# Splitting weights fewer tiles ahead in the mixers of a three-layer transformer on one core, with two gate steps a beat later and a shorter pooling matmul

## The reference

```python
for l in range(2):
    x = x + 0.5 * swiglu(rms_norm(x, ffn1_norm), ffn1_w_gate_up, ffn1_w_down)   # L0f1, L1f1
    z = rms_norm(x, mix_norm) @ w_in                     # L0, L1: u, q, k, v and two gates
    y_pool = multiscale_pool(u, pool_w, pool_scale)      # means over windows of 2, 4, 8, 16 tokens
    y_attn = attention(rope(rms_norm(q)), rope(rms_norm(k)), v)
    x = x + (gate0 * (y_pool @ w_branch_pool) + gate1 * (y_attn @ w_branch_attn)) @ w_out
    x = x + 0.5 * swiglu(rms_norm(x, ffn2_norm), ffn2_w_gate_up, ffn2_w_down)   # L0f2, L1f2
h = rms_norm(x, norm1_w) @ w_in_2                        # M
hm = mlstm_chunkwise(silu(conv(q, k)), v, i_pre, log_sigmoid(f_pre))   # q, k: Mqk; v: Mmv; mo: Mmo
on = gates * (compressed, selected and window attention)  # compress: 8 tiles Mkw1*, Mvw1*
x = x + (sigmoid(gm) * (hm @ w_up_m) + sigmoid(gn) * (on @ w_up_n)) @ w_out     # Mg, Mbr, Mwo
x = x + (gelu(conv(a)) * v) @ w_down                     # Mf
```

## Time and profile before

| | before |
|---|---|
| median of three runs | 1455.54 us |
| the profiled execution's own time | 1455.04 us |
| its span, first to last instruction | 1453.2 us |
| PE busy | 1441.2 us, 99% |
| DVE busy | 986.5 us, 68% |
| ACT busy | 820.1 us, 56% |
| POOL busy | 144.0 us, 10% |
| granted TensorE clock, mean | 0.999 |

### The profile page before, as it was taken

The page is one execution under the profiler, slowest core; times in us unless marked ns, Lnnn a source line. Parts: engine busy times, 40 slices in busy tenths (PEclk is TensorE's granted clock), DMA queues, the critical chain, the costliest instruction groups (busy, mean ns, idle before and its releaser), DMA issues.

```text
span 1453.2 us, 20919 instructions
## 1 busy us (share of the span) xinstructions
PE 1441.2 (99%) x8064; PEld 1235.0 (85%) x8064; DVE 986.5 (68%) x1604; ACT 820.1 (56%) x1414; POOL 144.0 (10%) x212
## 2 busy tenths in 40 slices
PE   9999999999999999999999999999998999999999
PEld 7888888798888888888887888888887899888887
DVE  6665676766666576666676677666676866778775
ACT  6555556754655555555557646555557665455553
POOL 0100023000000001000050003000049200100000
PEclk9999999999999999999999999999999999999999
DMA  8765555454656647655464456555546343456651
GB/s 330 248 196 195 181 204 181 138 182 169 214 183 193 197 142 234 193 187 191 161 228 159 150 170 216 186 194 186 186 152 249 120 139 132 159 173 220 196 188 51
DMA packets 73683, 267.78 MB, mean 184 GB/s; under 512 B 8176, under 2 KB 8304, under 8 KB 73456
## 3 DMA queue, kind: packets, MB, share of 16 engines
q1 hardware_dynamic: 73296, 265.65, 54.8%
q10 hardware_dynamic: 288, 0.79, 0.1%
HBM read 265.36 MB, written 1.05 MB: 183 GB/s over the span
## 4 chain that ended last, share of the span: by engine, by line
PE 96%; ACT 2%; DVE 1%; DMA 1%; issue 0%; SPq 0%
PE bank L545 29%; PE bank L550 15%; PE bank L498 8%; PE bank L499 8%; PE bank L500 8%; PE bank L559 4%; PE bank L564 4%; PE bank L560 4%; PE bank L528 3%; PE bank L535 3%; PE bank L529 3%; PE bank L518 1%; DMA raw<-w_dram 1%; PE bank L714 1%; PE bank L701 1%; PE bank L690 1%
## 5 line engine op out<-in xcount | busy, mean ns | idle before, releaser
L1558 DVE TENSOR_TENSOR wlo<-raw,whi 128x1024 fp32r<-128x1024 f32 (+1 forms) x481 | 578.5, 1225 | 18.1 <-ACT whi L1029 18.1
L1029 ACT ACTIVATE whi<-raw 128x1024 fp32r<-128x1024 f32 (+1 forms) x481 | 497.8, 1050 | 7.5 <-DMA raw<-w_dram 3.1
L545 PE MATMUL bank<-hx,whi 128*128 128x512 f32 x1856 | 468.7, 393 | 0.0
L545 PEld LDWEIGHTS bank<-hx,whi 128*128 128x128 f32 x1856 | 338.7, 189 | 66.2 <-issue 3.0
L550 PEld LDWEIGHTS bank<-hx,wlo 128*128 128x128 f32 x1856 | 253.3, 191 | 18.2
L550 PE MATMUL bank<-hx,wlo 128*128 128x256 f32 x1856 | 258.9, 283 | 0.0
L498 PE MATMUL bank<-whi,hid 128*128 128x512 f32 x536 | 211.5, 395 | 0.2 <-issue 0.2
L499 PE MATMUL bank<-wlo,hid 128*128 128x512 f32 x536 | 210.1, 392 | 0.0
L500 PE MATMUL bank<-whi,hid 128*128 128x512 f32 x536 | 208.9, 390 | 0.0
L1058 ACT ACTIVATE hid<-prod 128x256 fp32r<-128x256 f32 x126 | 52.7, 418 | 168.9 <-DVE prod L1662 109.0
L500 PEld LDWEIGHTS bank<-whi,hid 128*128 128x128 f32 x536 | 100.8, 188 | 21.8
(11 more groups left out here) (241 smaller groups left out, 1526.8 us busy)
## 6 DMA issues: line engine op xcount, KB each, us to landing
raw<-w_dram SPq DMA_DIRECT2D x486, 512.0 KB, 4.0
gain<-g_dram SPq DMA_DIRECT2D x7, 512.0 KB, 3.8
arena<-c_dram SPq DMA_DIRECT2D x2, 768.0 KB, 6.2
cst<-c_dram SPq DMA_DIRECT2D x1, 1056.0 KB, 6.4
out_dram<-x SPq DMA_DIRECT2D x4, 256.0 KB, 2.0
par<-p_dram SPq DMA_DIRECT2D x1, 867.0 KB, 8.0
raw<-w_dram SPq DMA_DIRECT2D x2, 432.0 KB, 3.6
gain<-g_dram ACTq DMA_DIRECT2D x1, 512.0 KB, 4.7
```

The lines of the kernel that those rows point to most:

```text
L545: e.matmul(b[:, :], hi_of(j)[:, k * P:k * P + P], hx[:, k * 2 * S:k * 2 * S + 2 * S], start=k == 0, stop=False, skip_group_check=True)
L1029: e.activation(hi_of(t), raw_of(t), ACT.Copy).then_inc(sem["w_hi"], 1)
L1558: e.tensor_tensor(lo_of(t), raw_of(t), hi_of(t).bitcast(F32), ALU.subtract).then_inc(sem["w_lo"], 1)
```

## The change

Four things are changed, no others. First, `HI_LEAD` and `LO_LEAD` give the leads tile by tile in the mixers. Second, the forget gates' columns (`gate_cols`) move from beat 29 to beat 30 on PE and DVE, and stand behind the attention of beat 29. Third, the transposes of the compressed attention's weights (`compressed` step 4, PE L913 and ACT L1395) move from beat 43 to 44. Fourth, the first pooling matmul of a group writes 130, 132, 136 or 144 columns in place of 256.

```diff
+MIXED_TILES = [f"Mqk{i}" if kind == "qk" else f"M{'kv'[i // 4]}w1{i % 4}" for kind, i in MIXED]
+HI_LEAD = dict(zip(MIXED_TILES, (3, 6, 6, 4, 3, 2, 1, 1, 3, 2, 2, 2)), Mmv0=2, Mmv2=3)
+LO_LEAD = dict(zip(MIXED_TILES, (3, 5, 5, 4, 3, 2, 1, 0, 1, 2, 1, 1)), Mmv0=1, Mmv2=1)
+for _t in ["Mmv4", "Mmv6"] + [f"Mmo{k}" for k in (0, 2, 4, 6)] + [f"Mg{j}{f}" for f in range(KD) for j in range(2)]:
+    HI_LEAD[_t], LO_LEAD[_t] = 4, 2
+HI_LEAD["Mg17"], LO_LEAD["Mg07"], LO_LEAD["Mg17"] = 5, 3, 4
+for _t in [f"L{l}g{j}{f}" for l in range(2) for f in range(KD) for j in range(2) if f or j]:
+    HI_LEAD[_t], LO_LEAD[_t] = 4, 3
...
-                    e.matmul(b[:, 0:S], us[:, g * P:g * P + P], pm[:, 0:S], start=True, stop=False, skip_group_check=True)
+                    reach = P + 2 ** (g + 1)
+                    e.matmul(b[:, 0:reach], us[:, g * P:g * P + P], pm[:, 0:reach], start=True, stop=False, skip_group_check=True)
...
-                    if beat == 29:
+                    attention(2, beat, 29, js, before)
+                    if beat == 30:
                         gate_cols()
-                    attention(2, beat, 29, js, before)
-                    if beat in (31, 34, 36, 38, 43):
-                        compressed((31, 34, 36, 38, 43).index(beat))
+                    if beat in (31, 34, 36, 38, 44):
+                        compressed((31, 34, 36, 38, 44).index(beat))
...
             def ahead(j):
-                hi_upto(min(j + AHEAD, len(plan) - 1))
+                hi_upto(min(j + HI_LEAD.get(plan[j][0], AHEAD), len(plan) - 1))
...
-                        hi_upto(T[f"Mqk{i}"] + 4)
+                        ahead(T[f"Mqk{i}"])
...
-                lo_upto(min(j + AHEAD - 1, len(plan) - 1))
+                lo_upto(min(j + LO_LEAD.get(plan[j][0], AHEAD - 1), len(plan) - 1))
```

More of the change, by code:

```diff
@@ L1448, in tick @@
                         compressed(3)
-                    if beat == 43:
+                    if beat == 44:
                         compressed(4)
@@ L1501, in mixer2 @@
                     if kind == "qk":
-                        hi_upto(T[f"Mqk{i}"] + 4)
+                        ahead(T[f"Mqk{i}"])
                         conv_in(i)
                     else:
-                        hi_upto(T[f"M{'kv'[i // 4]}w1{i % 4}"] + 4)
+                        ahead(T[f"M{'kv'[i // 4]}w1{i % 4}"])
                         tick()
@@ L2023, in tick @@
                         running_max()
-                    if beat == 29:
+                    attention(2, beat, 29, js)
+                    if beat == 30:
                         gate_cols()
-                    attention(2, beat, 29, js)
                     if beat == 36:
@@ L2067, in mixer2 @@
                     if kind == "qk":
-                        lo_upto(T[f"Mqk{i}"] + 3)
+                        ahead(T[f"Mqk{i}"])
                         conv_in(i)
                     else:
-                        lo_upto(T[f"M{'kv'[i // 4]}w1{i % 4}"] + 3)
+                        ahead(T[f"M{'kv'[i // 4]}w1{i % 4}"])
                         tick()
```

## The result

| | before | after |
|---|---|---|
| median | 1455.53 us (1455.38 to 1458.19, four runs) | 1446.93 us (1446.55 to 1447.16, four runs) |
| the profiled execution's own time | 1455.04 us | 1446.91 us |
| its span | 1453.2 us | 1445.1 us |

The ratio is 0.9938, with a 95% interval of 0.9926 to 0.9950 (the medians alone give 0.9941). The time lies 0.6 us under the predicted 1447.5 and inside the range.

A forecast was written before the change was run, and what follows sets the result against it. TensorE, busy 99% of the span, was taken as the bound. Terms of 4.8 (M), 0.1 (beat 44), 1.2 (L0, L1) and 1.6 (pooling) sum to 7.7 us off: 1447.5 us, 8-in-10 range 1445.2 to 1451.3.

The forecast's parts named there:

- The mechanism in M: In M, early-asked splits queue ahead of `sums` on DVE; new leads remove a 3.3 us wait and 1.7 us dip.
- Start of Mqk3: In M, `Mqk2`'s 0.5 us wait goes, `Mqk3`'s high part comes later; gain 0.35 us, between 0 and 0.8.
- The first `turn_p`: M's first pair: `sums` ready by 1114.2, PE there at 1115.25, so no wait; 3.3 us and the dip go.
- The second `turn_p`: In M, a new 1.2 us wait for ACT's `turned_p`, behind roundings; PE goes on at 1118.0 instead of 1122.78.
- M's term: Gain in M up to the second `turn_p`: -4.8 us (0.35 + 0.6 + 3.3 + 1.7 - 1.2).
- The fifth `turn_p`: After beat 44's transposes lose a 0.4 us wait, PE waits at the next `turn_p` instead: -0.1 us, between 0 and -0.6.
- L0, L1 and the pooling: L0 and L1 lose their `turn_p` waits, -1.2 us; pooling's first matmuls drop 964 columns in both layers, -1.6 us.
- Shorter leads by themselves: In M's gates, L0 and L1, later splits and loads are hidden by slack and cost nothing.
- The first (the clock falls again at the second `turn_p`): Rival in M: `turned_p` 1 to 2 us later, PE waits 2.2 to 3.2 us, dip returns: 1450.7; chance 0.17.
- The second (POOL's convolution late): Rival in M: slow POOL additions delay ACT's `conv_end`, price 0 to 2.6 us, middle 1448.8; chance 0.10.
- The third (low parts late in the gates): Rival at M's 16 `Mg` tiles: PE waits for low parts; 0.5 us each gives 1455.5; chance 0.03.
- The fourth: Rival in M: something unseen holds the chain, its term vanishes, 2.8 us are left: 1452.2; chance 0.08.

The follow-up runs named there:

- leads of 2 and 0: Changed kernel with the leads of M's first 14 gate tiles cut from 4 and 2 to 2 (high) and 0 (low): 1447.42 us.
- two low parts back: Changed kernel with the low parts' lead at `Mmv0` raised from 1 to 3: 1453.41 us.
- the better one: Changed kernel with the high parts' lead at `Mmv2` cut from 3 to 2 and the low parts' lead at `Mmo4` at 1: 1445.26 us.
- the short convolution: Kernel before with POOL's later convolution terms in M left out for 248 of 256 columns: 1452.21 us.

## Why the prediction was right

**The mechanism in M** was right: `sums` stood behind splits that were asked for too early, M's leads put that right (5.3 us alone by the medians, 4.8 by the marks), and the wait comes back when low parts are put back. I had the exponentials at 1110.4 on the old scale; less the 2.9 us that PE was ahead by then (1094.71 against 1091.78 at `Mqk1`'s start), this is 1107.5, and they came at 1106.95.

**Start of Mqk3:** 0.35 predicted. From `Mqk1`'s start it took 10.78 us before (1105.49 less 1094.71) and takes 10.40 now: 0.38. The number is right by luck. PE before, then after:

```profile
1099.73 0.38 PE L528 MATMUL bank<-hx,whi 128*128 128x256 f32 x1 [0.46 <-ACT whi L1029]
...
1101.60 0.66 PE L739 MATMUL bank<-cst,gates 128*128 128x128 f32 x4 [0.18 <-DVE gates L1876]
...
1104.06 1.50 PE L875 MATMUL bank<-raw,gates 128*32 128x256 f32 x24
```

```profile
1096.26 0.39 PE L536 MATMUL bank<-hx,whi 128*128 128x256 f32 x1
...
1100.21 1.50 PE L884 MATMUL bank<-raw,gates 128*32 128x256 f32 x24
```

From `Mqk1` to `Mqk2` PE takes 4.48 us for 5.02: 0.54 is won, the wait for `Mqk2`'s high part. From the last compression tiles to `Mqk3` it takes 1.97 us for 1.43: the 0.54 is given back in full, with a wait of 0.47 us for the late rounding. What stays is 0.38 us between (3.95 for 4.33), where `turn_q` (L739) no longer waits for DVE's L1876. The prediction doesn't name that wait.

**The first `turn_p`:** no wait, as predicted; the margin was 1.3 us.

**The second `turn_p`:** a new wait for `turned_p`, at the place and for the reason given, but of 0.7 us where 1.2 was predicted. ACT was 0.5 us earlier at the exponentials than I had it. This wait was mis-sized, and M's term came out at 5.1 us instead of 4.8 (8.07 us off at the second `turn_p`, less 2.93 at `Mqk1`'s start).

**The fifth `turn_p`:** a wait of 0.32 us for `sums` in place of the 0.42 at the transposes. The kernel is 8.19 us ahead there and was 8.07 at the second one: the 0.1 that was predicted.

**L0, L1 and the pooling:** predicted 1.2 and 1.6 us; 1.4 and 1.6 by the marks in the traces, 1.1 and 1.2 by the medians. **Shorter leads by themselves** cost nothing, as PE's timeline shows at M's last `turn_p`, before and after:

```profile
1213.24 0.49 PE L701 MATMUL bank<-cst,arena 128*128 128x128 f32 x3
```

```profile
1205.12 0.49 PE L709 MATMUL bank<-cst,arena 128*128 128x128 f32 x3
```

From the second `turn_p` it took 90.46 us before (1122.78) and takes 90.41 now (1114.71). Even leads of 2 and 0 cost only 0.5 us by the medians, 0.8 by the marks.

**The rivals.** The first (the clock falls again at the second `turn_p`) did not happen, but my reason against it was weak. I took 3.32 us of idle PE as what the dip needs, since shorter waits had none. With the old high leads the clock fell, in one execution of five, behind a wait of 1.34 us, which is 0.7 us more than what the change has and about what I had predicted for it (1.2). That no run of the change shows the fall may owe something to the wait being shorter than I had it. The second (POOL's convolution late) fell: POOL ended the first convolution at 1108.3, and ACT came to `conv_end` at 1111.9. The third (low parts late in the gates) is far off, by the run with leads of 2 and 0. The fourth fell by the windows.

## What to carry to other kernels

A lead fixed for all tiles puts splits that nobody needs yet in front of work that somebody waits for. Look for the first instruction of a chain in the engine's list, and ask for only as much ahead of it as the slack calls for. Test a small gain upstream in a kernel whose later waits are gone: on the kernel before, what the leads of L0 and L1 had won by 778 us vanished in a wait that ended at 1119.6 us.

## What was not expected

**The order in M also set how far runs differ.** The kernel before spread over 4.6 us in 27 runs, the kernels with only L's leads or only the pooling over 4.4 and 4.1 in 11 each, that with two low parts back over 2.5. The changed kernel spread over 0.6 us in four runs, the better one over 0.2 in five, the kernel before with the short convolution over 1.3 in nine. It isn't the long wait by itself: the kernel with only the beats moved waits 3.92 us in its profile, and its 11 runs lie within 1.0 us.

Much of the spread goes with the half clock, as the mean granted clock of each run of the kernel before shows:

| mean granted clock | runs (of 55, three sets) | us |
|---|---|---|
| 1.000 | 6 | 1453.38 to 1453.97 |
| 0.999 | 30 | 1453.64 to 1456.58 |
| 0.998 | 13 | 1455.44 to 1457.64 |
| 0.996 | 6 | 1457.58 to 1458.15 |

An estimate from these rows: 0.004 of 1453 us is 5.8 us of PE's work if PE is busy all that time, and the spread is 4.6. So the 1.7 us of the dip, which I took from one profile, are in most executions of the kernel before but not in all, and in some there is more. With the short convolution eight of nine runs have 1.000. Within one value of the clock up to 3 us remain, a part of them by rounding; what the stretched `sums` add, the runs don't separate.

**How long PE waits doesn't alone decide whether the clock falls.** In the kernel with the short pooling on the kernel before, the half clock came ahead of the `turn_p` wait, after one of 1.18 us at `gate_cols`, and none followed the 1.73 us at `turn_p`:

```profile
1107.11 0.39 PE L863 MATMUL bank<-cst,sil 128*128 128x4 f32 x2 [1.18 <-ACT sil L1373]
...
1118.73 0.55 PE L701 MATMUL bank<-cst,arena 128*128 128x128 f32 x3 [1.73 <-DVE arena L1722]
```

```profile
1109.15:1112.56 3.41, 3.41 (x15) 3.12 (x14) 3.34 (x13) 2.05 (x5) 3.25 (x4) 0.50 1.02 405
1116.80:1122.00 5.20, 3.47 (x26) 2.83 (x26) 5.06 (x12) 3.21 (x7) 5.04 (x8) 1.00 0.36 123
```

A wait of 1.34 us was followed by a fall in its profiled execution, one of 1.49 us (short convolution) was not. Single waits of up to 1.12 us (at 9.6 us in every profile) had none behind them in any profile of these kernels. What tells the cases apart was not tried.
